# The last pair of tiles of a hybrid block: gate products in another order, one tile finished on ScalarE, the other in quarters behind it

## What is computed

```python
x = x + (jax.nn.silu(gu[..., :D_FF]) * gu[..., D_FF:]) @ w_down[i]
gate = jax.nn.sigmoid(rmsnorm(x, g_ple_gate[i]) @ w_ple_gate[i])
e = rmsnorm(p[i] @ w_ple_up[i], g_ple_post[i])
x = x + gate * e
return rmsnorm(x, g_final)
```

## Time and profile before

| | |
|---|---|
| median of 3 runs | 1008.56 us (1008.4 to 1008.79) |
| the profiled execution | 1009.25 us |
| its span, first to last instruction | 1007.4 us |
| mean granted TensorE clock | 0.996 of full |
| busy: PE, DVE, ACT, POOL | 994.6, 754.1, 464.8, 385.8 us |
| moved by DMA | 138.25 MB |

### The profile page before, as it was taken

How to read it: one execution, slowest core, us unless ns; L and a number is a source line. 1 busy time by engine, 2 the same in 40 slices (tenths; PEclk the granted TensorE clock), 3 DMA queues, 4 the chain that set the end, 5 groups by cost and what they waited for, 6 DMA issues and landing times. The chain is left out here.

```text
span 1007.4 us, 12472 instructions
## 1 busy us (share of the span) xinstructions
PE 994.6 (99%) x4543; PEld 825.0 (82%) x4543; DVE 754.1 (75%) x1013; ACT 464.8 (46%) x713; POOL 385.8 (38%) x284
## 2 busy tenths in 40 slices
PE   8999999999999999999999999999999999999996
PEld 7888888888888888888888888888888888888785
DVE  5899999956699665665765764763677888885997
ACT  6724438504363333333333333333445665575764
POOL 3356797810146354354354454451000000011754
PEclk9999999999999999999999999999999999999998
DMA  7421102552213333332432432413998797533222
GB/s 254 137 84 42 66 19 104 210 167 84 105 55 101 118 105 87 123 105 76 133 105 73 136 105 65 145 64 108 353 379 307 236 312 256 190 103 105 85 101 87
DMA packets 103375, 138.25 MB, mean 137 GB/s; under 512 B 6107, under 2 KB 60915, under 8 KB 103315
## 3 DMA queue, kind: packets, MB, share of 16 engines
q1 hardware_dynamic: 103170, 137.21, 40.8%
q10 hardware_dynamic: 144, 0.26, 0.1%
HBM read 104.68 MB, written 32.77 MB: 136 GB/s over the span
## 5 line engine op out<-in xcount | busy, mean ns | idle before, releaser
L698 POOL TENSOR_SCALAR ss<-ss 128x1 f32<-128x1 f32 x38 | 17.7, 466 | 324.6 <-ACT junk L960 302.3
L2018 DVE SCALAR_TENSOR_TENSOR ps<-resid,convw,ps 128x512 f32<-128x512 f32 x190 | 127.4, 747 | 0.0
L1533 PE MATMUL ps<-ring_hi,ring_lo 128*128 128x512 f32 x308 | 120.0, 390 | 0.1
L1535 PE MATMUL ps<-ring_hi 128*128 128x512 f32 x308 | 119.8, 389 | 0.0
L1534 PE MATMUL ps<-ring_lo,ring_hi 128*128 128x512 f32 x308 | 119.8, 389 | 0.0
L1533 PE MATMUL ps<-act_hi,bs_lo 128*128 128x512 f32 x240 | 93.6, 390 | 0.0
L1535 PE MATMUL ps<-act_hi,bs_hi 128*128 128x512 f32 x240 | 93.4, 389 | 0.0
L1534 PE MATMUL ps<-act_lo,bs_hi 128*128 128x512 f32 x240 | 93.4, 389 | 0.0
L946 ACT ACTIVATE ring_hi<-raw 128x512 fp32r<-128x512 f32 x89 | 51.9, 625 | 60.4 <-PE ps L1535 60.4
L704 POOL TENSOR_TENSOR wc_lo<-raw_b,wc_hi 128x1024 fp32r<-128x1024 f32 x22 | 58.9, 2676 | 47.9 <-ACT wc_hi L946 46.7
L1931 DVE TENSOR_TENSOR ring_lo<-raw,ring_hi 128x512 fp32r<-128x512 f32 x89 | 58.0, 688 | 22.4 <-ACT ring_hi L946 22.3
(11 more groups left out here) (271 smaller groups left out, 2721.8 us busy)
## 6 DMA issues: line engine op xcount, KB each, us to landing
raw<-in_w_gate_up SPq DMA_DIRECT2D x44, 512.0 KB, 5.2
raw<-in_scratch SPq DMA_DIRECT2D x52, 256.0 KB, 3.4
raw<-in_w_down SPq DMA_DIRECT2D x52, 256.0 KB, 4.0
in_scratch<-in_s SPq DMA_DIRECT2D x44, 256.0 KB, 2.9
in_scratch<-gtmp SPq DMA_DIRECT2D x33, 256.0 KB, 2.3
keep<-in_w_down SPq DMA_DIRECT2D x32, 256.0 KB, 4.2
keep<-in_scratch SPq DMA_DIRECT2D x25, 256.0 KB, 3.6
resid<-in_x SPq DMA_DIRECT2D x8, 512.0 KB, 8.7
```

Source lines behind the costliest of these rows:

```text
L698: pool.tensor_scalar(ss[:, n:n + 1], ss[:, n:n + 1], 1.0 / D, EPS, ALU.mult, ALU.add)\
L1533: pe.matmul(dst, w_lo_, m_hi, start=start, stop=False, skip_group_check=onto)
L1535: return pe.matmul(dst, w_hi_, m_hi, start=False, stop=stop, skip_group_check=onto)
L2018: dve.scalar_tensor_tensor(out=conv_c if k == last_odd else acc, in0=u_all[:, c, k + h * BANK:k + (h + 1) * BANK], scalar=convw[:, c * 32 ...
```

## The change

It concerns only the last pair of tiles. The products run in the order 1, 2, 6, 5, 3, 7, 4. VectorE and ScalarE take both halves of tile 6 before C1 of tile 7. Tile 6 is no longer finished by VectorE's final: VectorE multiplies each half by the gain as soon as it is summed, into raw[:, 2, :], and ScalarE scales all of it by the factor in place; SP stores it from there. C1 of tile 7, which went that way before, now uses raw[:, 0, C0]. GpSimd makes tile 6's factor before it adds to tile 7's sum.

```diff
-        G_ORDER = (1, 2, 6, 5, 7, 3, 4)
+        G_ORDER = ((1, 2, 6, 5, 7, 3, 4), (1, 2, 6, 5, 3, 7, 4))
         def g_done(m, i):
-            return 7 * m + G_ORDER.index(i) + 1
+            return 7 * m + G_ORDER[m == PAIRS_G - 1].index(i) + 1
...
-            for t in range(4, TT - 1):
-                store_out(t)
+            store_out(4)
+            store_out(5)
+            sp.wait_ge(fin_act_ok, 1)
+            sp.dma_start(out_v[EVEN_ODD[TT - 2]], raw[:, 2, :]).then_inc(out_stored[0], DMA)
             t = TT - 1
-            sp.wait_ge(fin_ok, TT)
+            sp.wait_ge(fin_ok, TT - 1)
...
             pool.wait_ge(ss_ok, 3 * TT + 8)
-            pool.tensor_scalar(ss[:, n7:n7 + 1], ss[:, n7:n7 + 1], EPS, None, ALU.add).then_inc(ms_ok, 1)
-            pool.wait_ge(ss_ok, 3 * TT + 9)
             pool.tensor_scalar(ss[:, n6:n6 + 1], ss[:, n6:n6 + 1], ss[:, p6:p6 + 1], EPS, ALU.add, ALU.add)\
                 .then_inc(ms_ok, 1)
+            pool.wait_ge(ms_ok, 3 * TT + 7)
+            pool.tensor_tensor(rs[:, n6:n6 + 1], ss[:, n6:n6 + 1], neg_half[:, :], ALU.pow).then_inc(rs_ok, 1)
+            pool.wait_ge(ss_ok, 3 * TT + 9)
+            pool.tensor_scalar(ss[:, n7:n7 + 1], ss[:, n7:n7 + 1], EPS, None, ALU.add).then_inc(ms_ok, 1)
             pool.wait_ge(ms_ok, 3 * TT + 8)
-            pool.tensor_tensor(rs[:, n6:n6 + 1], ss[:, n6:n6 + 1], neg_half[:, :], ALU.pow).then_inc(rs_ok, 1)
...
             gate_p5(m)
-            sigmoid(3, c22_ok, QUADS + m + 1)
             act.wait_ge(e_sq, TT)
             act.wait_ge(res_ok, t)
             square_half(t - 1, C0, 4 * TT - 2, 3 * TT + 7)
             sigmoid(1, c12_ok, QUADS + m + 1)
             act.wait_ge(res_ok, t + 1)
-            square_half(t, C1, 4 * TT - 1, 3 * TT + 8)
+            square_half(t - 1, C1, 5 * TT, 3 * TT + 8)
+            sigmoid(3, c22_ok, QUADS + m + 1)
+            act.wait_ge(rs_ok, 4 * TT - 1)
+            act.wait_ge(xg_ok, 2)
+            out6 = raw[:, 2, :]
+            act.activation(out6, out6, ACT.Copy, scale=rs[:, 4 * TT - 2:4 * TT - 1]).then_inc(fin_act_ok, 1)
             sigmoid_21(m, CA)
             sigmoid_21(m, CB)
             act.wait_ge(res_ok, t + 2)
-            square_half(t - 1, C1, 5 * TT, 3 * TT + 9)
+            square_half(t, C1, 4 * TT - 1, 3 * TT + 9)
...
             act.wait_ge(rs_ok, 4 * TT)
-            act.wait_ge(xg_ok, 1)
-            last = raw[:, 2, C0]
+            act.wait_ge(xg_ok, 3)
+            last = raw[:, 0, C0]
...
-                gate_part(m, 7)
-                gate_part(m, 3)
-                gate_part(m, 4)
+                for i in G_ORDER[m == PAIRS_G - 1][4:]:
+                    gate_part(m, i)
...
             gated(t - 1, 4 * m + 1, t, C0)
+            dve.wait_ge(res_ok, t)
+            dve.wait_ge(gain_ok, 4)
+            times_final(raw[:, 2, C0], t - 1, C0)
+            gate_12(m)
+            gated(t - 1, 4 * m + 2, t + 1, C1)
+            dve.wait_ge(res_ok, t + 1)
+            times_final(raw[:, 2, C1], t - 1, C1)
             gate_22(m)
-            gated(t, 4 * m + 2, t + 1, C1)
-            gate_12(m)
-            dve.wait_ge(res_ok, t + 1)
-            dve.wait_ge(gain_ok, 4)
-            dve.tensor_tensor(raw[:, 2, C0], x_tile(t, 3)[:, C1], pair(2)[:, C1], ALU.mult).then_inc(xg_ok, 1)
-            gated(t - 1, 4 * m + 3, t + 2, C1)
+            gated(t, 4 * m + 3, t + 2, C1)
             gated(t, 4 * m + 4, t + 3, CA)
             gated(t, 4 * m + 5, t + 4, CB)
-            final(t - 1)
+            dve.wait_ge(res_ok, t + 2)
+            times_final(raw[:, 0, C0], t, C1)
             final(t, C0)
```

More of the change, by code:

```diff
@@ L1522, in _ @@
             act.wait_ge(rs_ok, 4 * TT)
-            act.wait_ge(xg_ok, 1)
-            last = raw[:, 2, C0]
+            act.wait_ge(xg_ok, 3)
+            last = raw[:, 0, C0]
             act.activation(last, last, ACT.Copy, scale=rs[:, 4 * TT - 1:4 * TT]).then_inc(fin_act_ok, 1)
-            act.wait_ge(fin_act_ok, 1)
+            act.wait_ge(fin_act_ok, 2)
             act.dma_start(out_v[EVEN_ODD[t]][:, C1], last).then_inc(out_stored[1], DMA)
@@ L2434, in _, with times_final @@
             final(t - 2)
+            def times_final(dst, t, c):
+                dve.tensor_tensor(dst, x_tile(t, 3)[:, c], pair(2)[:, c], ALU.mult).then_inc(xg_ok, 1)
             gated(t - 1, 4 * m + 1, t, C0)
-            gate_22(m)
-            gated(t, 4 * m + 2, t + 1, C1)
-            gate_12(m)
-            dve.wait_ge(res_ok, t + 1)
-            dve.wait_ge(gain_ok, 4)
-            dve.tensor_tensor(raw[:, 2, C0], x_tile(t, 3)[:, C1], pair(2)[:, C1], ALU.mult).then_inc(xg_ok, 1)
-            gated(t - 1, 4 * m + 3, t + 2, C1)
+            dve.wait_ge(res_ok, t)
[5 more added lines that the diff above has]
+            times_final(raw[:, 2, C1], t - 1, C1)
+            gate_22(m)
+            gated(t, 4 * m + 3, t + 2, C1)
             gated(t, 4 * m + 4, t + 3, CA)
             gated(t, 4 * m + 5, t + 4, CB)
-            final(t - 1)
+            dve.wait_ge(res_ok, t + 2)
+            times_final(raw[:, 0, C0], t, C1)
             final(t, C0)
```

## The result

The changed kernel takes 1013.09 us in the median of six runs (1011.17 to 1013.2), the kernel before 1008.53 (1008.4 to 1009.12). The medians lie 4.6 us apart; the ratio, which takes in the one run at 1011.17 as well, is 1.0040, with a 95% interval from 1.0029 to 1.0051: slower by some 4 us, a small loss, but clear of no change. The likeliest case of the forecast, 1010.6 us, didn't come; rival A did, in most runs. The forecast ran from 1009.8 to 1013.0 us: the ratio, applied to its 1008.56 us, gives 1012.6 and lies inside, the median 0.1 us above.

The account below looks back on a forecast made before the run. TensorE's products, busy 99% of the span, were taken to bound the kernel. +3.65 for product 4's start, -0.88 behind the products and -0.70 for the stores gave +2.07 us: 1010.6 us, range 1009.8 to 1013.0.

Parts of the forecast that it names:

- rival A: Last pair, before product 4: the clock falls in or shortly behind TensorE's idle; +4.2 us in sum, 1012.7 us; chance 0.30.
- the two waits: TensorE in the last pair: about 1.1 us before product 3 for ScalarE's copy, 2.4 us before product 4 for gate_22.
- the term of +3.65: Product 4 of the last pair, waiting for gate_22 in VectorE's list, starts at 998.77 instead of 995.12: +3.65 us.
- the first wait: Product 3 waits about 1.1 us for ScalarE's copy of product 5's bank; covered by VectorE's chain, so removing it gives nothing.
- a fall of the clock: Over product 4: granted clock was to stay 1.00, matmuls 0.227 us apart; the prediction is wrong if it falls.
- The term of -0.88: Behind the last matmul, the quarter CA of tile 7 comes after 0.43 us instead of 1.31: -0.88 us.
- moves alike: The median of the runs, 1008.56 us, 0.7 below the profiled execution, shifts by the same +2.07 us, to 1010.6.
- stores -1.0 to 0: Landing of the last stores, 512 KB together instead of 1 MB: -0.7 us taken, bounds -1.0 and 0.
- restart 0.05 to 0.5: TensorE's restart before product 4 after waiting for gate_22: 0.12 us taken, bounds 0.05 and 0.5.
- the line of 1010.6: Forecast time and limit of about 0.2%, 2.0 us, between no change and slower; slower got 0.63, within 0.2% 0.34.
- B: VectorE's add at 991.08 isn't held by GpSimd's multiply, so its chain starts earlier: +1.35 us, 1009.9 us; chance 0.07.
- C: Product 4 doesn't depend on gate_22, so only the wait before product 3 stays: +0.9 us, 1009.5 us; chance 0.03.

Follow-up runs that it names:

- the add's freedom: The changed kernel with the gated product of C0 of tile 6 in a free PSUM bank instead of SBUF: 1010.91 us, ratio 1.0021.
- both edits together: The changed kernel with the gated product of C0 of tile 6 in PSUM and gate_22 one place earlier in VectorE's list: ratio 1.0015, 1010.3 us.

## Why the prediction was right and wrong

**The direction and the mechanism of the two waits were right.** Both came where they were put. The second was added up from rows of before to start product 4 at 998.77; the changed kernel, 0.12 us ahead as a whole, started it at 998.69, so the term of +3.65 measured +3.69. gate_22 one place earlier moved it by 0.73 and the add's freedom by 0.47, so the list and its two ends are shown. That the first wait is covered was argued, and the rows bear it out, with some 0.5 us to spare; the run that shortened the wait moved something else too.

**The clock was judged wrong.** The forecast had named a fall of the clock as a sign of being wrong, and it came. Rival A had the mechanism and a row for it, a fall 2.2 us after the last matmul, and got 0.30; by times and mean clocks it happened in eight of eleven runs. The step that failed is the weighing, "whether matmuls that come back after 2.4 us keep the clock, no row shows": coming back didn't keep it. In the profiled execution the fall came 1.3 us after TensorE had resumed, 3.5 us after it had stopped. That row of before was no measure of when the clock falls, though: in the ten profiled executions that kept the clock through product 4, it fell between 2.2 us (the kernel before) and 5.3 us (both edits together) after the last matmul. From one row neither 0.30 nor its opposite could be had. The price of the fall was set too high: 2.1 us were taken, 1.31 measured (4.34 less 3.03 us for product 4), near the 1.35 that the text gave for a fall in product 4's middle. The Trainium skill's example (TensorE: Matmul & The Clock Gate, Loop structure matters more than you think), 8 us of idle before every matmul, says nothing of shorter idles; that "by it alone this shorter gap is free" didn't follow, and 2.2 us were enough here.

**Behind the products.** The term of -0.88 measured -0.86 (0.45 us from the last matmul to the quarter CA). From there to the last issue it is 4.35 us against 4.28. Product 4 at full clock takes 3.03 us, not the 2.89 carried over: from its first matmul after the wait to the next are 0.31 us, and the later ones take 0.23. The last store lands in 2.7 us, a gain of 0.6 where 0.7 were taken. The Trainium skill's fixed 2.0 us and 436 GB/s (DMA: Bandwidth & Descriptors, Anatomy of one DMA) are given for transfers issued by GpSimd; the estimate from them, 3.2 us, doesn't fit these stores of SP and ScalarE, and the row was the better guide.

**The sum.** In the profiled executions: +3.69 for the start of product 4, +0.14 for its length, +1.31 for the clock, -0.86, +0.07, -0.6 for the landing, and -0.12 for the shift: +3.6, as the spans say (1007.4 to 1011.0). Two more terms make the 4.6 us between the medians, and the forecast had neither. Around the span lie 1.8 to 1.9 us in every run of the kernel before and of the four versions built on it, and 2.1 to 2.2 us in every run with the changed lists, whatever the order of its products: +0.3 us, which no row explains. And the median of before lay 0.7 us below its profiled execution, that of the changed kernel 0.1 below its own: "moves alike" was off by 0.6 us. The profiled execution of before was one whose last pair began late (990.16, against 989.25 to 989.66 in the four versions built on it).

**The range.** Its own terms (stores -1.0 to 0, restart 0.05 to 0.5) give the forecast 1010.3 to 1011.7 us, not 1009.9 to 1011.4. More than half of that lies above the line of 1010.6, so "slower" deserved more than its 0.63. That A's 1012.7 us came within 0.4 of the median is in part luck: the clock was priced 0.8 us too high, and the two missing terms, 0.9 us together, made up for it.

**Rivals B and C.** B's premise didn't come (the add was held for 2.76 us); done by hand it gave 0.47 us of its 0.7, as product 3 lets gate_12 go later than reckoned, and through the clock far more. C falls: product 4 does wait for gate_22. Tile 6's scaling never stood in the way.

## What to carry to other kernels

When an accumulation is put directly behind the product whose bank has to be read out first, count the reader's whole list from its last fixed point; here that list put product 4 off by 3.7 us, where the reader itself takes 0.7. Before accepting an idle of a few microseconds on TensorE, price the work behind it at half clock too; where nothing better can fill the gap, matmuls without use may, as nine did here for 1.3 us. Where a VectorE add is held beside a long GpSimd operation, try one operand in PSUM: it took the add here from 2.77 to 0.69 us.

## What the runs showed of the hardware

- The granted clock stayed at 2.4 GHz over product 4, by times and mean clocks (0.997 or more), in all 22 runs with 1.5 or 1.7 us of idle in front of it and in the eight with 1.0; with 2.2 us it fell in eight of eleven, 1.3 us after work had resumed in one profiled execution and 1.2 us in the other; with 4.4 us it fell just before the work resumed and was back 3.4 us later.
- Behind the last matmul the clock fell after 2.2 to 5.3 us, in ten profiled executions that had kept it until then. One such row says little about the next.
- VectorE's add with both operands in SBUF, begun 0.4 us after GpSimd's multiply, ended 0.55 us after it (2.76 us in all); with one operand in PSUM it took 0.69 us beside the same multiply. A gated multiply with two SBUF operands was held likewise, 2.59 us, when it came second, and ran in 0.75 us when it came first.
- Half a megabyte stored as two halves from two queues landed in 2.5 to 2.8 us; with another half megabyte issued 0.6 to 0.8 us ahead, in 3.0 to 3.4.
